# Two spectra and three norms: the second filters' folds and the sums of squares moved to VectorE

## The chip, the cores and the metric

The kernel runs on one core of a Trainium2 chip. The metric is the device time of one execution in microseconds, the median over the runs. All times below are microseconds unless marked ns. Engines: PE is TensorE, DVE is VectorE, ACT is ScalarE, POOL is GpSimd, SP is SyncE.

## What is computed

Two blocks of two layers each, all in float32, over 512 tokens of width 1024 and 256 context tokens. Both layers of the first block are attention layers with three kinds of heads. In the second block layer 0 (the "even" layer) joins a gated linear recurrence with long convolutions, layer 1 is a conformer convolution, and each is followed by 16 experts that choose their tokens. Ahead of every layer, of the experts and of the output stands a norm:

```python
def _rmsnorm(x, g):
    xf = x.astype(jnp.float32)
    y = xf * lax.rsqrt(jnp.mean(xf * xf, axis=-1, keepdims=True) + EPS)
    return (y * g.astype(jnp.float32)).astype(x.dtype)
```

The long convolutions of the even layer go through spectra, twice, each time with a filter of its own (o is 0 and 1) that a small network makes:

```python
def _fftconv(u, kf, bias):
    n = u.shape[1]
    uf = u.astype(jnp.float32)
    y = jnp.fft.irfft(jnp.fft.rfft(uf, n=2 * n, axis=1) * kf[None], n=2 * n, axis=1)[:, :n]
    return (y + uf * bias.astype(jnp.float32)).astype(u.dtype)
...
    z = v
    for o in range(HYENA_ORDER):
        z = gates[o] * _fftconv(z, kf[:, o], p['filt_bias'][o])
```

## The kernel before

The program is written by hand, engine by engine, with semaphores. Activations lie with channels on the partitions: XC holds the state (8 tiles of 128 channels by 768 tokens), HT the normed input of a layer. TensorE writes its results into two large PSUM buffers, BIG0 and BIG1, in turn; each use waits until the use before the last has been freed (`big_free`). A float32 matmul of 512 columns stands in the trace as two records of 128x512.

**A norm** (`norm`, `root_of_mean` on ScalarE, `norm_sums`, `square_sums`, `all_sums` on TensorE). While a layer's output projection runs, VectorE adds each tile, gated, to XC (`add_gated`, L1870; for four tiles of the even layer L2177), and ScalarE squares the tile into HT (L1471). TensorE sums the squares over the channels in groups of 32 output rows (`square_sums`), ScalarE copies that to RS (L1480), TensorE sums once more with ones (L863 for 512 columns, L865 for the 256 of the context), ScalarE takes the logarithm (L1483) and the exponential (L1487), VectorE scales (L1860) and ScalarE adds the shift (L1494). `keep_clock` puts matmuls without use between (L804). The norm behind the first attention layer has 768 tokens, those behind the second and behind the even layer 512.

**The spectra** (`even_layer`). The transform of real input is made in an even and an odd half, for two groups g of frequencies and two waves, cosine and sine, so in four matmul groups of 1024 columns, one use of BIG each (`transform`). "Folding" adds and subtracts the halves. TensorE's order is:

- filters and their spectrum for o = 0, filters for o = 1;
- the signal's spectrum (four uses), then the spectrum of the filters for o = 1 (four uses, the raw halves), since the tables are loaded then;
- four transforms back (`back_to_tokens`), the first of which waits for three of four spectral products (`spec_ready`), the third for the fourth;
- the signal to tokens again, the signal's spectrum (four uses), a part of the output projection into other banks (`partial`), four transforms back.

For the signal's spectrum ScalarE copies the even half to TA (`first_halves`, L1662) and VectorE folds it with the odd half in PSUM (`fold`, L2118 and L2119). After all four folds VectorE makes four products of ten operations each (`signal_spectrum`, L2139 to L2149), for g and half 0 and 1. Behind every transform back it adds and gates (`back_to_tokens`, L2158 and L2161).

The raw halves for o = 1 go from BIG to UT, a buffer in HT, by ScalarE (`raw_spectrum`, L1680), and from there GpSimd folds them (L742, L743) into two other places, in the weight ring and in the context part of XC, which the products of o = 1 read. UT holds two at a time, so ScalarE waits for GpSimd from the third on, and again before UT takes the signal's tokens.

The deleted lines of the diff below show these folds.

SyncE loads the weights in units of 1 MiB into a ring; a load waits for `unit_used`, which TensorE raises with the first matmul after a unit's last use (`mm`). The stage of the experts streams its weights through a ring of 16 such units.

## Time and profile before

| what | value |
|---|---|
| median of three runs | 3146.27 us (3146.1 to 3153.19) |
| the profiled execution, its own time | 3150.18 us |
| its span, first to last instruction | 3148.1 us |
| PE busy | 2958.5 us, 94% |
| DVE busy | 1236.6 us, 39% |
| ACT busy | 781.8 us, 25% |
| POOL busy | 92.9 us, 3% |
| mean granted clock of TensorE | 0.985 of full speed |

The profile counts an engine as busy while one of its instructions runs. A row of the timeline gives the start, the busy time, engine, line, operation, tiles and shapes, and in brackets how long the engine had been idle and what released it. Rows of one line that follow each other are merged ("x16"), and then the busy time is that of all. The granted clock is 1.00 at 2.4 GHz and 0.50 at 1.2 GHz. The even layer's spectra lie between 1730 and 1876 us, the three norms that are changed at 874, 1512 and 1917 us.

### The profile page before, as it was taken

Reading aid. Unit: us, or ns where it says so; the run is one execution under the profiler, and the core shown is the slowest. Engines: PE = TensorE matmul, PEld = TensorE weight load, DVE = VectorE, ACT = ScalarE, POOL = GpSimd, SP = SyncE. Lnnn points to the kernel's source line nnn. Section 1 sums busy time; section 2 is a strip of 40 time slices with the busy share of each in tenths; the row PEclk is TensorE's granted clock in tenths of the full one; section 3 lists DMA queues with packets and bytes.
Section 4 is the critical chain, followed back from the end, with each engine's and each line's share of the span. In section 5 each row is a group of like instructions: output and inputs, shape, how many; then the busy total and the mean of one; then the engine's idle time right before and its main releaser. Section 6 shows DMA issues by size and latency. Waiting matters only on the chain.

```text
span 3148.1 us, 33763 instructions
## 1 busy us (share of the span) xinstructions
PE 2958.5 (94%) x13428; PEld 1535.1 (49%) x13428; DVE 1236.6 (39%) x2397; ACT 781.8 (25%) x1370; POOL 92.9 (3%) x164
## 2 busy tenths in 40 slices
PE   7999988999999989999998799999999998999998
PEld 3556555655555555554443354444443434444442
DVE  1455564675024556681356653111112543111112
ACT  3223444332022245341343102010012122010011
POOL 0000000000000000010000100000000000000000
PEclk9999999999999999999999999999999999999999
DMA  6222221223112323233111014999997224999996
GB/s 263 72 92 72 79 87 61 68 79 122 67 53 100 125 90 125 87 122 136 54 67 40 15 67 187 410 421 421 422 420 305 73 76 172 405 421 421 421 421 283
DMA packets 90525, 584.47 MB, mean 186 GB/s; under 512 B 10176, under 2 KB 10176, under 8 KB 29216
## 3 DMA queue, kind: packets, MB, share of 16 engines
q1 hardware_dynamic: 69696, 502.56, 39.9%
q0 software_dynamic: 20704, 80.16, 7.9%
q8 instruction: 89, 1.46, 0.2%
q14 instruction: 36, 0.29, 0.0%
HBM read 580.58 MB, written 2.10 MB: 185 GB/s over the span
## 4 chain that ended last, share of the span: by engine, by line
PE 84%; DVE 9%; ACT 5%; issue 1%; DMA 1%; DVEq 0%; SPq 0%; ACTq 0%; POOL 0%
PE BIG L755 46%; PE PJ L755 21%; PE BIG L1412 4%; PE PJ L1010 3%; PE PT L989 3%; PE BIG L972 2%; PE BIG L976 1%; DVE SPILL L1845 1%; ACT ARENA L1572 1%; ACT ARENA L1562 1%; DVE STAT L1981 1%; PE PT L755 1%; PE PT L1388 0%; DMA W<-in_units 0%; ACT ARENA L1517 0%
## 5 line engine op out<-in xcount | busy, mean ns | idle before, releaser
L755 PE MATMUL PJ<-HT,W 128*128 128x512 f32 (+1 forms) x1792 | 648.0, 515 | 22.6 <-ACT ARENA L1544 11.0
L755 PE MATMUL BIG<-ARENA 128*64 128x512 f32 (+1 forms) x2368 | 474.3, 465 | 4.8 <-DVE ARENA L2266 2.5
L755 PEld LDWEIGHTS PJ<-HT,W 128*128 128x128 f32 x1792 | 337.3, 193 | 279.2 <-issue 240.5
L755 PEld LDWEIGHTS BIG<-ARENA 128*64 128x64 f32 (+1 forms) x2368 | 236.2, 165 | 230.7 <-issue 223.9
L755 PE MATMUL BIG<-HT,W 128*128 128x512 f32 (+1 forms) x768 | 321.0, 579 | 5.5 <-DVE CONST L2027 3.6
L755 PE MATMUL BIG<-W,ARENA 128*64 128x512 f32 (+1 forms) x1280 | 285.6, 576 | 18.4 <-DVE ARENA L2149 18.3
L755 PE MATMUL BIG<-ARENA,W 128*128 128x512 f32 (+1 forms) x768 | 289.7, 539 | 1.5 <-ACT ARENA L1729 1.5
L1572 ACT ACTIVATE ARENA<-PT 128x512 f32<-128x512 f32 (+1 forms) x280 | 150.0, 571 | 467.8 <-PE PT L989 466.5
L2295 DVE SCALAR_TENSOR_TENSOR XC<-BIG,MOD,XC 128x512 f32<-128x512 f32 x128 | 90.2, 747 | 379.6 <-PE BIG L1412 379.6
L755 PEld LDWEIGHTS BIG<-HT,W 128*128 128x128 f32 x768 | 146.8, 192 | 177.3 <-issue 166.5
L1845 DVE CUSTOM_DVE_ANT_0 SPILL<-W,VEC 128x1024 bf16<-128x1024 f32 x168 | 215.2, 1281 | 7.6 <-DMA W<-in_mod_rows 1.6
L755 PEld LDWEIGHTS BIG<-ARENA,W 128*128 128x128 f32 x768 | 145.7, 190 | 143.9 <-issue 138.2
L755 PEld LDWEIGHTS BIG<-W,ARENA 128*64 128x64 f32 (+1 forms) x1280 | 110.1, 144 | 179.6 <-issue 172.6
L1562 ACT ACTIVATE ARENA<-BIG,STAT 128x768 f32<-128x768 f32 (+6 forms) x240 | 174.0, 730 | 61.4 <-DVE STAT L1981 60.6
L1981 DVE TENSOR_REDUCE STAT<-BIG 128x1 f32<-128x768 f32 (+6 forms) x240 | 174.1, 742 | 29.0 <-PE BIG L976 24.0
L989 PE MATMUL PT<-CONST,ARENA 128*128 128x128 f32 x1056 | 155.8, 282 | 17.3 <-ACT ARENA L1572 16.1
L755 PE MATMUL BIG<-HT,ARENA 128*64 128x512 f32 x576 | 169.7, 592 | 0.0
L1010 PEld LDWEIGHTS PJ<-ARENA 128*64 128x64 f32 x2112 | 113.9, 136 | 84.3 <-issue 46.8
L1010 PE MATMUL PJ<-ARENA 128*64 128x128 f32 x2112 | 142.9, 278 | 9.9 <-DVE ARENA L1890 4.4
L989 PEld LDWEIGHTS PT<-CONST,ARENA 128*128 128x128 f32 x1056 | 112.1, 140 | 72.1 <-issue 38.6
L1935 DVE TENSOR_SCALAR ARENA<-ARENA,STAT 128x512 f32<-128x512 f32 (+3 forms) x240 | 123.5, 515 | 8.4
L1412 PE MATMUL BIG<-ARENA 128*128 128x512 f32 x256 | 115.0, 602 | 0.0
(254 smaller groups left out, 2188.9 us busy)
## 6 DMA issues: line engine op xcount, KB each, us to landing
ARENA<-in_exp_w SPq DMA_DIRECT2D x168, 1024.0 KB, 18.2
W<-in_exp_w SPq DMA_DIRECT2D x144, 1024.0 KB, 16.8
W<-in_units SPq DMA_DIRECT2D x89, 1024.0 KB, 4.9
HT<-in_exp_w SPq DMA_DIRECT2D x72, 1024.0 KB, 22.0
W<-in_mod_rows POOLq DMA_DIRECT2D x128, 512.0 KB, 3.9
ARENA<-in_bias_b POOLq DMA_DIRECT2D x16, 448.0 KB, 5.6
XC<-in_x SPq DMA_DIRECT2D x1, 3072.0 KB, 10.3
W<-in_mod_vectors POOLq DMA_DIRECT2D x2, 1024.0 KB, 6.2
```

The lines of the kernel that those rows point to most:

```text
L755: ins = pe.matmul(out, lhsT, rhs, start=start, stop=stop)
L972: pe.matmul(BIG[h][:, N - (b - a) * P:N], Q[rows, i % 2, t * P:t * P + P], keys[rows, a * P:b * P], start=True, stop=True)
L976: pe.matmul(BIG[h][:, N:NA], Q[rows, i % 2, t * P:t * P + P], keys[rows, N:NA], start=True, stop=True).then_inc(scores_filled, 1)
L989: last = pe.transpose(PT[:, a:a + P], PROB[:, h, y * P:y * P + P], const("ident"))
L1010: last = pe.matmul(PJ[use_o[0]][head * HD:head * HD + HD, 0:P], V[:, buf_of[i], tile, head * HD:head * HD + HD], PTS[:, at:at + P], start= ...
L1412: last = pe.matmul(BIG[k_use % 2][:, half * N:half * N + N], YK[:, m * P:m * P + P], GSCAT[:, :], start=True, stop=True)
L1562: act.activation(PROB[:, h, 0:b - a], BIG[h][:, a:b], ACT.Exp, bias=STAT[:, c:c + 1], accum_out=STAT[:, 4 + c:5 + c]).then_inc(probs_exp, 1)
L1572: act.activation(PTS[:, a:a + w], PT[:, bank:bank + w], ACT.Copy).then_inc(t_copied, 1)
L1845: dve.tensor_tensor_reduce(SPILL[:, :], MODW[:, row % 2, :], MODV[:, which, :], 1.0, vec("mod_b", at), ALU.mult, ALU.add, MOD[:, at:at + 1 ...
L1935: dve.tensor_scalar(probs, probs, STAT[:, 8 + c:9 + c], None, ALU.mult)\
L1981: dve.tensor_reduce(STAT[:, c:c + 1], out[:, a:b], AX.X, ALU.max, negate=True).then_inc(max_ready, 1)
L2295: ins = dve.scalar_tensor_tensor(XC[:, m, 0:N], BIG[k_use % 2][:, half * N:half * N + N], mod(group, 5, m, 0), XC[:, m, 0:N], ALU.mult, AL ...
```

## The change

It has two parts.

**Folds.** ScalarE evicts the raw halves straight to the two places in the weight ring and in XC (now RAW_COS and RAW_SIN), without waits on another engine. GpSimd's folds are deleted. VectorE folds them (`fold_raw`) behind the four gatings of o = 0, into KR and KS, the places of the first filters' spectrum, so both products read the same tiles. `signal_spectrum` folds group 0, makes the first product, and only then folds group 1; it does so for both o.

**Norms.** For the three norms named above VectorE adds up the squares in HT as they come (`add_squares`): behind the gating of tile m it adds the square of tile m-2 (the sum so far) to that of tile m-1. TensorE sums only two tiles, the running sum and the last square, with ones of full width (`summed_squares`). The copy to RS and the second sum go. The other norms stay.

```diff
         LRU_W = W[:, RING, :].rearrange("p (g n) -> p g n", n=P)
-        SPEC_R1 = W[:, RING, :].rearrange("p (g s w n) -> p g w s n", g=2, s=2, w=2)
-        SPEC_S1 = XC[:, :, N:NA].rearrange("p (g s w) n -> p g w s n", g=2, s=2)
+        RAW_COS = W[:, RING, :].rearrange("p (g s w n) -> p g s w n", g=2, s=2, w=2)
+        RAW_SIN = XC[:, :, N:NA].rearrange("p (g s w) n -> p g s w n", g=2, s=2)
         FILT_W3 = W[:, RING + 1, :]
...
         DFT_IN, DFT_OUT = (W[:, hyena_slots[x], :].rearrange("p (a k b) -> p a k b", a=4, k=2) for x in (1, 2))
-        SPECTRA = [[x.rearrange("p g s (w n) -> p g w s n", w=2) for x in (KR, KS)], [SPEC_R1, SPEC_S1]]
+        SPECTRUM = [x.rearrange("p g s (w n) -> p g w s n", w=2) for x in (KR, KS)]
...
-            for x in range(4):
-                g, wave = divmod(x, 2)
-                even, odd = (UT[:, 2 * (x % 2) + part, :].rearrange("p (w n) -> p w n", w=2) for part in range(2))
-                plus, minus = (SPECTRA[1][wave][:, g, :, s, :] for s in range(2))
-                pool.wait_ge(raw_copied, x + 1)
-                pool.tensor_tensor(plus, even, odd, ALU.add)
-                pool.tensor_tensor(minus, odd if wave else even, even if wave else odd, ALU.subtract)\
-                    .then_inc(raw_folded, 1)
...
+            def summed_squares(n):
+                k_use = me.next_big()
+                pe.wait_ge(big_free[k_use % 2], me.over(k_use - 2))
+                out = BIG[k_use % 2]
+                for k in (KT - 2, KT - 1):
+                    if k == KT - 2:
+                        pe.wait_ge(squares_added, me.next("squares_added"))
+                        me.next("squares", KT)
+                    else:
+                        pe.wait_ge(squares, me.seen["squares"])
+                    last = mm(out[:, 0:N], const("ones"), HT[:, k, 0:N], k == KT - 2, k == KT - 1)
+                if n > N:
+                    for k in (KT - 2, KT - 1):
+                        last = pe.matmul(out[:, N:n], const("ones"), HT[:, k, N:n], start=k == KT - 2, stop=k == KT - 1)
+                last.then_inc(big_filled, 1)
...
                     act.activation(HT[:, k, 0:n], XC[:, k, 0:n], ACT.Square).then_inc(squares, 1)
-                root_of_mean(n)
+                root_of_mean(n, summed)
                 if shift is not None:
...
-            def root_of_mean(n):
-                k_use = me.next_big()
-                act.wait_ge(big_filled, me.fills(k_use))
-                act.activation(RS[:, 0:n], BIG[k_use % 2][:, 0:n], ACT.Copy).then_inc(big_free[k_use % 2], 1)
+            def root_of_mean(n, summed=False):
+                if not summed:
+                    k_use = me.next_big()
+                    act.wait_ge(big_filled, me.fills(k_use))
+                    act.activation(RS[:, 0:n], BIG[k_use % 2][:, 0:n], ACT.Copy).then_inc(big_free[k_use % 2], 1)
                 k_use = me.next_big()
...
                 act.activation(RS[:, 0:n], BIG[k_use % 2][:, 0:n], ACT.Ln, bias=EPSC[:, 0:1],
-                               scale=1.0 / (32 * D))\
+                               scale=1.0 / (D if summed else 32 * D))\
                     .then_inc(big_free[k_use % 2], 1)
...
                     for x in range(4):
+                        g, wave = divmod(x, 2)
+                        raw = (RAW_COS, RAW_SIN)[wave][:, g].rearrange("p s w n -> p (s w) n")
                         k_use = me.next_big()
                         act.wait_ge(big_filled, me.fills(k_use))
-                        if x >= 2:
-                            act.wait_ge(raw_folded, x - 1)
-                        act.activation(UT[:, 2 * (x % 2):2 * (x % 2) + 2, :],
-                                       BIG[k_use % 2][:, :].rearrange("p (a b) -> p a b", b=N), ACT.Copy)\
+                        act.activation(raw, BIG[k_use % 2][:, :].rearrange("p (a n) -> p a n", n=256), ACT.Copy)\
                             .then_inc(big_free[k_use % 2], 1)
-                        act.wait_ge(big_free[k_use % 2], me.over(k_use)).then_inc(raw_copied, 1)
...
                 me.big += 4
-                act.wait_ge(raw_folded, 4)
                 signal_tokens()
...
-            def norm(n, weight, group, scale_chunk, dst, done):
+            def add_squares(n, m, before):
+                if m >= 2:
+                    dve.wait_ge(squares, before + m)
+                    ins = dve.tensor_tensor(HT[:, m - 1, 0:n], HT[:, m - 1, 0:n], HT[:, m - 2, 0:n], ALU.add)
+                    if m == KT - 1:
+                        ins.then_inc(squares_added, 1)
+                    else:
+                        link(ins)
+            def norm(n, weight, group, scale_chunk, dst, done, summed=False):
...
                                                       1.0, weight, ALU.add, ALU.mult))
-                me.big += 2
+                me.big += 1 if summed else 2
                 dve.wait_ge(rs_ready, me.next("rs_ready"))
...
                     ins.then_inc(big_free[k_use % 2], 1)
+                    add_squares(n, m, before)
...
-                def signal_spectrum(o):
-                    for g in range(2):
+                def fold_raw(first_use):
+                    for x in range(4):
+                        g, wave = divmod(x, 2)
+                        even, odd = ((RAW_COS, RAW_SIN)[wave][:, g, s, :, :] for s in range(2))
+                        plus, minus = ((KR, KS)[wave][:, g, s, :].rearrange("p (w n) -> p w n", w=2) for s in range(2))
+                        dve.wait_ge(big_free[(first_use + x) % 2], me.over(first_use + x))
+                        dve.tensor_tensor(plus, even, odd, ALU.add)
+                        ins = dve.tensor_tensor(minus, odd if wave else even, even if wave else odd, ALU.subtract)
+                    link(ins)
+                def signal_spectrum():
+                    def folds(g):
...
+                    folds(0)
                     for g in range(2):
                         for half in range(2):
+                            if (g, half) == (0, 1):
+                                folds(1)
                             part = slice(half * 256, half * 256 + 256)
-                            kr, ks = (SPECTRA[o][wave][:, g, half, :, :] for wave in range(2))
+                            kr, ks = (SPECTRUM[wave][:, g, half, :, :] for wave in range(2))
                             ur, us, zt, zr = (x[:, :, part] for x in (UR[g], US[g], ZT, ZR))
...
                 filters()
-                signal_spectrum(0)
+                signal_spectrum()
+                first_use = me.big
                 me.big += 4
                 back_to_tokens(0)
+                fold_raw(first_use)
                 me.big += 2
-                dve.wait_ge(raw_folded, 4)
-                signal_spectrum(1)
+                signal_spectrum()
                 back_to_tokens(1)
...
                                              ALU.mult, ALU.add).then_inc(partial_added, 1)
-                add_gated(N, lambda m, c: mod(2, 2, m, c), range(4, KT))
+                    add_squares(N, m, SQUARES_BEFORE["even"])
+                add_gated(N, lambda m, c: mod(2, 2, m, c), SQUARES_BEFORE["even"], range(4, KT))
```

What moves on the engines shows in the orders. First VectorE at the signal's spectrum of o = 0, before, from the second of its four pairs of folds (L2118, L2119) to the start of the first product (L2139, L2140); UR, US and KR lie in ARENA:

```order
L2118 TENSOR_TENSOR ARENA<-ARENA,BIG1 128x512 [waits half_copied,big_free0]
L2119 TENSOR_TENSOR ARENA<-BIG1,ARENA 128x512
L2118 TENSOR_TENSOR ARENA<-ARENA,BIG0 128x512 [waits half_copied,big_free1]
L2119 TENSOR_TENSOR ARENA<-ARENA,BIG0 128x512
L2118 TENSOR_TENSOR ARENA<-ARENA,BIG1 128x512 [waits half_copied,big_free0]
L2119 TENSOR_TENSOR ARENA<-BIG1,ARENA 128x512
L2139 TENSOR_TENSOR ARENA<-ARENA 128x2x256 [waits big_free1]
L2140 TENSOR_TENSOR ARENA<-ARENA 128x2x256
```

And in the changed kernel, the end of the first product (L2183 to L2186), the second two pairs of folds (L2139 and L2140 there), and the start of the second product (L2176):

```order
L2183 TENSOR_TENSOR ARENA<-ARENA 128x256 [waits dve_chain]
L2184 TENSOR_TENSOR ARENA<-ARENA 128x256
L2185 TENSOR_TENSOR ARENA<-ARENA 128x256
L2186 TENSOR_TENSOR ARENA<-ARENA 128x256
L2139 TENSOR_TENSOR ARENA<-ARENA,BIG0 128x512 [waits half_copied,spec_ready]
L2140 TENSOR_TENSOR ARENA<-ARENA,BIG0 128x512
L2139 TENSOR_TENSOR ARENA<-ARENA,BIG1 128x512 [waits half_copied,big_free0]
L2140 TENSOR_TENSOR ARENA<-BIG1,ARENA 128x512
L2176 TENSOR_TENSOR ARENA<-ARENA 128x2x256 [waits big_free1]
L2177 TENSOR_TENSOR ARENA<-ARENA 128x2x256
```

The two folds of group 1, which free BIG0 and BIG1 for the raw transforms, have moved behind ten operations. The second place is VectorE between the last gating of o = 0 and the next signal spectrum, before:

```order
L2158 SCALAR_TENSOR_TENSOR ARENA<-ARENA,VEC,BIG0 128x2x256 [waits big_filled]
L2161 TENSOR_TENSOR ARENA<-ARENA 128x512 [waits dve_chain]
L2158 SCALAR_TENSOR_TENSOR ARENA<-ARENA,VEC,BIG1 128x2x256 [waits big_filled]
L2161 TENSOR_TENSOR ARENA<-ARENA 128x512 [waits dve_chain]
L2118 TENSOR_TENSOR ARENA<-ARENA,BIG0 128x512 [waits half_copied,raw_folded]
L2119 TENSOR_TENSOR ARENA<-ARENA,BIG0 128x512
```

and in the changed kernel (L2195 and L2198 are the gating, L2157 and L2158 the new folds, W and XC where the raw halves lie):

```order
L2195 SCALAR_TENSOR_TENSOR ARENA<-ARENA,VEC,BIG1 128x2x256 [waits big_filled]
L2198 TENSOR_TENSOR ARENA<-ARENA 128x512 [waits dve_chain]
L2157 TENSOR_TENSOR ARENA<-W 128x512 [waits big_free0]
L2158 TENSOR_TENSOR ARENA<-W 128x512
L2157 TENSOR_TENSOR ARENA<-XC 128x512 [waits big_free1]
L2158 TENSOR_TENSOR ARENA<-XC 128x512
L2157 TENSOR_TENSOR ARENA<-W 128x512 [waits big_free0]
L2158 TENSOR_TENSOR ARENA<-W 128x512
L2157 TENSOR_TENSOR ARENA<-XC 128x512 [waits big_free1]
L2158 TENSOR_TENSOR ARENA<-XC 128x512
L2139 TENSOR_TENSOR ARENA<-ARENA,BIG0 128x512 [waits half_copied,dve_chain]
```

Eight additions of 512 columns now stand there. The third place is TensorE at the norm behind the first attention layer (PJ and BIG are PSUM, CONST holds the ones), before:

```order
L755 MATMUL BIG<-ARENA,W 128x256 x12
L755 MATMUL BIG<-HT,CONST 32x512 x8
L755 MATMUL BIG<-HT,CONST 32x256 x8
L863 MATMUL BIG<-ARENA,CONST 128x512
L865 MATMUL BIG<-ARENA,CONST 128x256
L804 MATMUL PJ<-CONST 128x512 x5
L755 MATMUL PJ<-HT,W 128x512 x8
```

and in the changed kernel:

```order
L748 MATMUL BIG<-ARENA,W 128x256 x12
L748 MATMUL BIG<-HT,CONST 128x512 x2
L845 MATMUL BIG<-HT,CONST 128x256 x2
L797 MATMUL PJ<-CONST 128x512 x5
L748 MATMUL PJ<-HT,W 128x512 x8
```

Sixteen narrow sums and two wide ones have become four wide ones.

## Rows read from the trace of the kernel before

**Rows 1.** The page, busy time of each engine.
```profile
PE 2958.5 (94%) x13428; PEld 1535.1 (49%) x13428; DVE 1236.6 (39%) x2397; ACT 781.8 (25%) x1370; POOL 92.9 (3%) x164
```
**Rows 2.** Timeline of VectorE, first signal spectrum: start, busy time, engine, line, operation, tiles.
```profile
1775.10 0.68 DVE L2119 TENSOR_TENSOR ARENA<-BIG,ARENA 128x512 f32<-128x512 f32 x1
...
1782.67 0.69 DVE L2139 TENSOR_TENSOR ARENA<-ARENA 128x512 f32<-128x512 f32 x1
...
1785.34 1.75 DVE L2143 TENSOR_TENSOR ARENA<-ARENA 128x512 f32<-128x512 f32 x1
...
1801.84 0.69 DVE L2139 TENSOR_TENSOR ARENA<-ARENA 128x512 f32<-128x512 f32 x1
...
1807.41 0.69 DVE L2139 TENSOR_TENSOR ARENA<-ARENA 128x512 f32<-128x512 f32 x1
```
**Rows 3.** Timeline of GpSimd, first and last of its eight folds.
```profile
1785.24 1.30 POOL L742 TENSOR_TENSOR W<-HT 128x512 f32<-128x512 f32 x1 [240.89 <-ACTq L1683]
...
1796.75 1.71 POOL L743 TENSOR_TENSOR XC<-HT 128x512 f32<-128x512 f32 x1
```
**Rows 4.** Timeline of all engines, first spectrum and the transforms back.
```profile
1780.65 0.60 ACT L1662 ACTIVATE ARENA<-BIG 128x512 f32<-128x512 f32 x1 [2.84 <-PE BIG L755]
...
1807.52 16.29 PE L755 MATMUL BIG<-W,ARENA 128*128 128x256 f32 x64 [13.17 <-DVE ARENA L2149]
...
1813.56 0.75 DVE L2158 SCALAR_TENSOR_TENSOR ARENA<-ARENA,VEC,BIG 128x512 f32<-128x512 f32 x1 [0.61 <-PE BIG L755]
...
1816.94 0.75 DVE L2158 SCALAR_TENSOR_TENSOR ARENA<-ARENA,VEC,BIG 128x512 f32<-128x512 f32 x1 [1.91 <-PE BIG L755]
...
1823.85 0.75 DVE L2158 SCALAR_TENSOR_TENSOR ARENA<-ARENA,VEC,BIG 128x512 f32<-128x512 f32 x1 [1.98 <-PE BIG L755]
...
1831.92 0.69 DVE L2118 TENSOR_TENSOR ARENA<-ARENA,BIG 128x512 f32<-128x512 f32 x1 [6.60 <-ACT ARENA L1662]
```
**Rows 5.** Windows: stretch, its length, busy time by engine, granted clock, DMA share, GB/s.
```profile
1807.50:1811.00 3.50, 3.48 (x8) 2.83 (x9) 3.40 (x6) 0.00 (x0) 0.00 (x0) 0.50 0.30 61
```
**Rows 6.** Timeline of the second spectrum, VectorE's second fold, and the transforms back.
```profile
1835.96 0.68 DVE L2119 TENSOR_TENSOR ARENA<-BIG,ARENA 128x512 f32<-128x512 f32 x1
...
1860.38 15.47 PE L755 MATMUL BIG<-W,ARENA 128*128 128x256 f32 x64 [5.16 <-DVE ARENA L2149]
...
1875.89 0.75 DVE L2158 SCALAR_TENSOR_TENSOR ARENA<-ARENA,VEC,BIG 128x512 f32<-128x512 f32 x1 [1.98 <-PE BIG L755]
```
**Rows 7.** Timeline of the norm with 768 tokens; last, VectorE's group of 768 columns.
```profile
874.16 1.14 DVE L1870 SCALAR_TENSOR_TENSOR XC<-BIG,MOD,XC 128x512 f32<-128x512 f32 x2 [14.34 <-PE BIG L755]
...
875.33 0.84 ACT L1471 ACTIVATE HT<-XC 128x768 f32<-128x768 f32 x1 [14.64 <-DVE XC L1870]
...
879.04 1.13 PE L863 MATMUL BIG<-ARENA,CONST 128*128 128x512 f32 x2 [0.90 <-ACT ARENA L1480]
...
880.63 0.90 ACT L1483 ACTIVATE ARENA<-BIG,EPSC 128x768 f32<-128x768 f32 x1 [0.35 <-PE BIG L865]
...
L2047 DVE TENSOR_TENSOR ARENA<-ARENA 128x768 f32<-128x768 f32 x8 | 7.7, 958 | 8.3 <-ACT ARENA L1633 8.2
```
**Rows 8.** Timeline of the norm behind the second attention layer, 512 tokens.
```profile
1512.60 0.75 DVE L1870 SCALAR_TENSOR_TENSOR XC<-BIG,MOD,XC 128x512 f32<-128x512 f32 x1 [9.55 <-PE BIG L755]
...
1515.80 1.13 PE L863 MATMUL BIG<-ARENA,CONST 128*128 128x512 f32 x2 [0.69 <-ACT ARENA L1480]
...
1517.06 0.69 ACT L1483 ACTIVATE ARENA<-BIG,EPSC 128x512 f32<-128x512 f32 x1
```
**Rows 9.** Timeline of TensorE, two gaps elsewhere.
```profile
1294.56 5.85 PE L755 MATMUL PJ<-HT,W 128*128 128x512 f32 x13 [2.33 <-DVE ARENA L1952]
...
1658.14 1.79 PE L1030 MATMUL BIG<-ARENA,W 128*128 128x512 f32 x2 [2.29 <-ACT ARENA L1625]
```
**Rows 10.** The experts: SyncE's queue behind the even layer, and a window of the stage.
```profile
1918.43 26.12 SPq L633 DMA_DIRECT2D ARENA<-in_exp_w  x7
...
2025.00:2075.00 50.00, 50.00 (x254) 22.55 (x250) 5.07 (x7) 5.55 (x6) 0.00 (x0) 1.00 1.01 420
```

More of the change, by code:

```diff
@@ L192, in unit_order @@
     return first, second
+SQUARES_BEFORE = {"attention": [KT, 2 * KT], "even": 4 * KT}
 class Count:
@@ L479, in build @@
         squares = sem("squares")
+        squares_added = sem("squares_added")
         rs_ready = sem("rs_ready")
@@ L525, in build @@
         y_half_copied = sem("y_half_copied")
-        raw_copied = sem("raw_copied")
-        raw_folded = sem("raw_folded")
         partial_done = sem("partial_done")
@@ L1436, in _ @@
             attention(0)
-            norm_sums(NA)
+            summed_squares(NA)
             keep_clock(5)
             attention(1)
-            norm_sums(N)
+            summed_squares(N)
             keep_clock(4)
@@ L1444, in _ @@
             even_layer()
-            norm_sums(N)
+            summed_squares(N)
             keep_clock(4)
@@ L1459, in _, with norm @@
             me = Count()
-            def norm(n, updates, shift, follow=None):
+            def norm(n, updates, shift, follow=None, summed=False):
                 for k in range(KT):
@@ L1800, in _ @@
             updates = attention(0)
-            norm(NA, updates, lambda k, c: mod(1, 0, k, c))
+            norm(NA, updates, lambda k, c: mod(1, 0, k, c), summed=True)
             updates = attention(1)
-            norm(N, updates, None)
+            norm(N, updates, None, summed=True)
             act.wait_ge(ctx2_loaded, 16)
@@ L1807, in _ @@
             updates = even_layer()
-            norm(N, updates, lambda k, c: mod(2, 3, k, c))
+            norm(N, updates, lambda k, c: mod(2, 3, k, c), summed=True)
             updates = experts(0)
@@ L1861, in norm, with add_gated @@
                                                  ALU.mult, ALU.mult).then_inc(done, 1)
-            def add_gated(n, gates, tiles=range(KT)):
+            def add_gated(n, gates, before, tiles=range(KT)):
                 for m in tiles:
@@ L1945, in attention @@
                 dve.wait_ge(mod_made, MODS_DONE[0])
-                add_gated(nq, lambda m, c: mod(layer, 2, m, c))
+                add_gated(nq, lambda m, c: mod(layer, 2, m, c), SQUARES_BEFORE["attention"][layer])
             def values(kv, part, use):
@@ L2316, in _ @@
                     dve.wait_ge(mod_made, MODS_DONE[1])
-                norm(NA, vec("norm_w", 8 * layer, 8), layer, 1, HT, h_scaled)
+                norm(NA, vec("norm_w", 8 * layer, 8), layer, 1, HT, h_scaled, summed=layer == 1)
                 attention(layer)
-            norm(N, vec("final_norm_w", 0, 8), None, None, XC, block_done)
+            norm(N, vec("final_norm_w", 0, 8), None, None, XC, block_done, summed=True)
             dve.wait_ge(block_done, KT)
@@ L2332, in _ @@
             even_layer()
-            norm(N, vec("norm2_g", 0, 8), 2, 4, HT, h_scaled)
+            norm(N, vec("norm2_g", 0, 8), 2, 4, HT, h_scaled, summed=True)
             experts(0)
```

## The prediction

> **What bounds the kernel now.** I read the page first: TensorE is busy for 2958.5 us of a span of 3148.1 us [rows 1]. Work taken off another engine therefore counts only where TensorE stands still for it. The second view is the timeline of VectorE, GpSimd, ScalarE and TensorE around the two signal spectra and around each norm; the third is the same stretch in windows, for the granted clock. The two edits touch five places: the first and second spectrum, and three norms. Times below are those of the trace of before.
>
> **First spectrum, before.** VectorE folds the four signal transforms as they arrive and then makes four products of ten operations. The third product takes from 1801.84 to 1807.41, 5.57 us [rows 2]. The first two together take from 1782.67 to 1801.84, 19.17 us, where two at 5.57 are 11.14: 8.03 us are lost. The long operations (1.75 us at 1785.34, where its like takes 0.69) stand exactly where GpSimd folds the raw halves, 1785.24 to 1798.46 [rows 2, 3]. TensorE must have three products: it has nothing to do for 13.17 us and goes on at 1807.52 [rows 4]. The clock granted in the 3.5 us behind that is 0.50, the lower level of 1.2 GHz [rows 5]. In the end four transforms back, 3.455 us apart at full speed (1816.94 to 1823.85), need 16.33 us from 1807.52 to the eviction of the fourth, where 4 x 3.455 + 0.1 = 13.9 would do.
>
> **First spectrum, changed.** GpSimd's folds are gone, so every product costs 5.57 us. The order is new too: the first product is made before the second pair of folds. The second fold ends at 1775.10 + 0.68 = 1775.78 [rows 2]. Then: product 1 to 1781.35; two folds of 0.61 + 0.68 to 1783.95; products 2 and 3 to 1795.1; product 4 to 1800.7. This adds a wait. The buffer of the third transform is freed by its fold at 1782.65, and TensorE wants it for the first raw transform when the fourth is done, at 1780.55 (ScalarE copies its half at 1780.65) [rows 4]. So TensorE stalls for 2.2 us, and behind it stand the four raw transforms, now ending at 1807.52 - 13.17 = 1794.35 and then at 1796.55. That is later than the third product (1795.1), so TensorE itself is what comes last, and it goes on at 1796.6: 10.9 us earlier. Without the 13 us of standing still the clock should stay up, so 16.33 becomes 13.9: 2.4 us more. **Gain 13.3 us.** The fourth product (1800.7) delays nothing: the third transform back, which needs it, starts at 1803.5.
>
> **The folds, now on VectorE.** Eight additions of 512 columns at 0.61 us apart (0.69 at most, from the two rows of a fold) are 4.9 to 5.6 us. They follow the last gating; there VectorE has been idle for 6.60 us before 1831.92 [rows 4]. Hidden, cost 0, with 1.0 to 1.7 us to spare. If that cover were gone, each microsecond would delay the second spectrum. ScalarE loses three waits and no work: a copy of 1024 columns to another place. GpSimd loses eight operations that nothing else follows on its queue.
>
> **Second spectrum.** Only the order changes. The second fold ends at 1836.64 [rows 6]; product 1 to 1842.2, folds to 1844.8, products 2 and 3 to 1856.0. TensorE goes on then, at 1856.1, not at 1860.38; it has been free since 1860.38 - 5.16 = 1855.2. That is 4.3 us. From 1860.38 to the fourth eviction at 1875.89 are 15.51 us, against 13.9 at full speed: 1.6 us more if 0.9 us of waiting leaves the clock alone. The fourth product ends at 1861.6, so the first gating frees its buffer at 1863.2, 0.2 us after the third transform could have started. **Gain 5.7 us.**
>
> **Three norms.** Before, ScalarE's last square is followed by sums on TensorE, a copy, a second sum and the logarithm. With 768 tokens the last gating ends at 875.30 and the logarithm starts at 880.63 [rows 7]. Now VectorE adds squares behind each gating; the six additions ahead of the last hide in the 14 us between gatings. The last, of 768 columns, takes 0.96 us (the nearest row, L2047) and ends at 876.28; the last square runs beside it, 875.33 to 876.17. TensorE starts at 876.36. Now 879.04 to 880.63, 1.59 us, is one sum of 512 and one of 256 columns with the way to ScalarE. Columns of 512 are two records of 0.43 us, those of 256 half as much, so two sums each need 1.59 + 0.86 + 0.43 = 2.88 us: logarithm at 879.24. **Gain 1.4 us.** With 512 tokens the gating ends at 1513.35, the addition at 1514.05, TensorE starts at 1514.15 and needs 1.26 + 0.86 = 2.12 us: 1516.27 instead of 1517.06 [rows 8]. **Gain 0.8 us, twice.** The matmuls that keep the clock up end 1.5 us sooner with the rest, so they don't become the bound. ScalarE's table load of 1.28 us stays under TensorE's sums.
>
> One DMA is moved with it: the release of the last output unit hangs on the first sum, which now waits for the additions. The loads of expert weights that follow it started at 1918.43 [rows 10], before the last gating ended at 1917.84 + 0.69; they will start about 1 us later against the gating. The queue issues these seven over 26.12 us and a microsecond hides in that; cost 0.
>
> **Sum.** 13.3 + 5.7 + 1.4 + 0.8 + 0.8 = 22.0 us. Against it stand two new gaps of 2.2 us on TensorE, at the first raw transform and ahead of the sums of the norm with 768 tokens. Of such gaps the trace shows both kinds: after 2.33 us at 1294.56 records come 0.45 us apart (5.85 us for 13); after 2.29 us at 1658.14 two records take 1.79 us [rows 9]. A fall costs about 1.7 us if it lasts as long as the 3.5 us at half speed in [rows 5], nothing if only the matmuls that keep the clock up run in it. I take one fall of the two, -1.7 us: **20.3 us gained**. The Trainium skill, "TensorE: Matmul & The Clock Gate", section "HAM oscillation", lets the clock fall only after longer standing still than these gaps; by that rule the sum would be 22.0. The row at 1658.14 speaks against it, so I keep 20.3.
>
> The profiled execution took 3150.18 us, its span 3148.1; it is 3.9 above the median of the runs, 3146.27, whose own spread is 7 us. It would become 3129.9, the median **3126.0 us**.
>
> **Rivals.**
> The products stay slow (0.07): it may be ScalarE's evictions of the four raw transforms that slow VectorE, not GpSimd. For it: they lie in the same stretch. Against it: the slow operations stop with GpSimd's last, and the gatings and folds of the second spectrum, with ScalarE evicting between them, run at full speed. Then the third product ends 8.0 us later, at 1803.1, TensorE stands for 6.6 us, the clock falls as before, and the first spectrum gains 4.3: 13.0 in all, 3133.3 us. The Trainium skill, "SBUF — State Buffer", section "Who interferes with whom", has only VectorE and GpSimd share a port; by it this rival would have no chance.
>
> The folds don't hide (0.05): were the eight additions as slow as the long ones (1.65 us), they would need 13.2 us against 6.6 of cover, and 6.6 come back: 15.4 less 1.7 gained, 3132.6 us. Nothing but GpSimd made them slow, so it is unlikely.
>
> The experts take it back (0.06): beside them the DMA queues are full (share 1.01, 420 GB/s) while TensorE is busy for 50.00 of 50 us [rows 10]. If the stream of weights set the end, it would still start with the same release, which comes some 19 us earlier; lost are the last norm's 0.8 and the 1 us of delay: 3127.8 us.
>
> Slower (0.02): the clock. If the fall behind a new gap did not end after some microseconds but held through the stretch of attention or of the transforms that follows, then each microsecond at 1.2 GHz loses half of one. To end 9.4 us above before it must eat 22.0 + 9.4 = 31.4 us, that is 63 us at the lower level: about 3156 us. From 44 us on the gain is gone. The 3.5 us of [rows 5] are the kind of length that the trace has, so this is a remote case.
>
> No change worth the name (0.03): a mix of these with a late wait that I don't see, say another operand of the transforms back; the gain of the first spectrum would be lost, 3139 us or more.
>
> **Numbers.** A measurement can tell about 0.3%, 9.4 us. My case has 0.77 and lies between 3124 (no fall) and 3128 (two). The range takes in the 22.0 with some microseconds of the runs' spread below, and the first rivals above: 3120.5 to 3133.5. Faster by over 0.3% (under 3136.8) is 0.95, within it 0.03, slower 0.02.
>
> **What would show it.** Right: all products at 5.6 us; TensorE's wait ahead of the transforms back gone in the first spectrum and about 1 us in the second; a new wait of 2.2 us at the first raw transform, released by a fold; eight additions between the last gating and the next fold with 1 to 2 us idle behind; the logarithm 3.9 us after the last gating with 768 tokens, 2.9 us with 512. Wrong: products above 0.7 us per operation with GpSimd idle, a TensorE wait over 2 us ahead of the transforms back, or stretches at 1.2 GHz behind the new gaps that last longer than those of before.

## The result and the profile after

Seven runs of the changed kernel have a median of 3133.2 us (3127.32 to 3141.46); seven of the kernel before, on the same chip and in turn with them, 3153.19 us (3145.71 to 3154.79). The first three of these seven are the three behind the median of 3146.27 us that the prediction started from. The ratio is 0.9946, 95% interval 0.993 to 0.9962: 17 us less, 12 to 22. The profiled execution took 3131.21 us with a span of 3129.2; that of the kernel before took 3150.18 with a span of 3148.1, 19 us more.

The page of the changed kernel, span and busy time of each engine, against [rows 1]:

```profile
span 3129.2 us, 33675 instructions
## 1 busy us (share of the span) xinstructions
PE 2951.6 (94%) x13372; PEld 1532.3 (49%) x13372; DVE 1245.7 (40%) x2423; ACT 779.8 (25%) x1367; POOL 81.2 (3%) x156
```

TensorE is busy 6.9 us less and the span is 18.9 us shorter: most of what went was standing still.

**First spectrum.** Timeline of VectorE, ScalarE and TensorE in the changed kernel; columns are start, busy time, engine, line, operation and tiles, in brackets the idle time before and what ended it. L2139 and L2140 are the folds of the signal, L2176 the first operation of a product, L2195 a gating, L2157 and L2158 the folds of the raw halves. The rows are picked from the three engines, so rows between them are left out:

```profile
1775.35 0.68 DVE L2140 TENSOR_TENSOR ARENA<-BIG,ARENA 128x512 f32<-128x512 f32 x1
1776.07 0.69 DVE L2176 TENSOR_TENSOR ARENA<-ARENA 128x512 f32<-128x512 f32 x1
1781.64 0.69 DVE L2139 TENSOR_TENSOR ARENA<-ARENA,BIG 128x512 f32<-128x512 f32 x1
1782.98 14.00 PE L748 MATMUL BIG<-HT,W 128*128 128x512 f32 x32 [2.11 <-DVE ARENA L2140]
1784.29 0.69 DVE L2176 TENSOR_TENSOR ARENA<-ARENA 128x512 f32<-128x512 f32 x1
1789.86 0.69 DVE L2176 TENSOR_TENSOR ARENA<-ARENA 128x512 f32<-128x512 f32 x1
1795.44 0.69 DVE L2176 TENSOR_TENSOR ARENA<-ARENA 128x512 f32<-128x512 f32 x1
1796.82 13.98 PE L748 MATMUL BIG<-W,ARENA 128*128 128x256 f32 x64
1810.83 0.75 DVE L2195 SCALAR_TENSOR_TENSOR ARENA<-ARENA,VEC,BIG 128x512 f32<-128x512 f32 x1 [1.98 <-PE BIG L748]
1812.22 0.68 DVE L2157 TENSOR_TENSOR ARENA<-W 128x512 f32<-128x512 f32 x1
1816.44 0.69 DVE L2158 TENSOR_TENSOR ARENA<-XC 128x512 f32<-128x512 f32 x1
```

Products start 5.57 us apart (1784.29, 1789.86, 1795.44), where the first two took 19.17 together [rows 2]. TensorE no longer stands still ahead of the transforms back: its row at 1796.82 has no bracket, where [rows 4] have 13.17 us. In its place is the wait of 2.11 us at the first raw transform, ended by a fold (the third of the signal's four, the one at 1781.64). From the start of the second fold (1775.35, before 1775.10) to the fourth gating (1810.83, before 1823.85) are 35.48 us instead of 48.75: **13.27 us gained**.

**Second spectrum.** The same views, from the first fold on the signal to the fourth gating:

```profile
1818.84 0.69 DVE L2139 TENSOR_TENSOR ARENA<-ARENA,BIG 128x512 f32<-128x512 f32 x1 [1.71 <-ACT ARENA L1674]
1822.88 0.68 DVE L2140 TENSOR_TENSOR ARENA<-BIG,ARENA 128x512 f32<-128x512 f32 x1
1843.07 14.17 PE L748 MATMUL BIG<-W,ARENA 128*128 128x256 f32 x64 [0.94 <-DVE ARENA L2186]
1857.28 0.75 DVE L2195 SCALAR_TENSOR_TENSOR ARENA<-ARENA,VEC,BIG 128x512 f32<-128x512 f32 x1 [1.98 <-PE BIG L748]
```

The eight new additions leave VectorE idle for 1.71 us, where it had 6.60 [rows 4]: they are hidden. TensorE waits for 0.94 us instead of 5.16 [rows 6]. Second fold to fourth gating is 34.40 us, before 1875.89 - 1835.96 = 39.93: **5.53 us gained**.

**The norms.** With 768 tokens; L1890 is the gating, L1862 the addition of squares, L1495 the logarithm:

```profile
874.39 1.14 DVE L1890 SCALAR_TENSOR_TENSOR XC<-BIG,MOD,XC 128x512 f32<-128x512 f32 x2 [13.47 <-PE BIG L748]
875.45 0.95 DVE L1862 TENSOR_TENSOR HT<-HT 128x768 f32<-128x768 f32 x1
876.55 3.08 PE L748 MATMUL BIG<-HT,CONST 128*128 128x512 f32 x4 [2.26 <-DVE HT L1862]
879.42 1.64 PE L845 MATMUL BIG<-HT,CONST 128*128 128x256 f32 x4
881.10 0.90 ACT L1495 ACTIVATE ARENA<-BIG,EPSC 128x768 f32<-128x768 f32 x1 [3.39 <-PE BIG L845]
```

The same, with 512 tokens (the norm behind the second attention layer):

```profile
1512.89 0.75 DVE L1890 SCALAR_TENSOR_TENSOR XC<-BIG,MOD,XC 128x512 f32<-128x512 f32 x1 [8.95 <-PE BIG L748]
1514.38 1.96 PE L748 MATMUL BIG<-HT,CONST 128*128 128x512 f32 x4 [1.60 <-DVE HT L1862]
1516.38 0.69 ACT L1495 ACTIVATE ARENA<-BIG,EPSC 128x512 f32<-128x512 f32 x1 [0.77 <-PE BIG L748]
```

With 512 tokens the logarithm starts 3.49 us after the start of the gating, before 1517.06 - 1512.60 = 4.46 [rows 8]: 0.97 us gained, and as much at the norm behind the even layer. With 768 tokens it starts after 6.71 us, before 880.63 - 874.16 = 6.47 [rows 7]: **0.24 us lost**. The four records of 512 columns that take 1.96 us at 1514.38 take 3.08 at 876.55. The window shows why; columns are the stretch, its length, busy time of PE, PEld, DVE, ACT and POOL with the instructions of each, the granted clock, the DMA share and GB/s:

```profile
877.00:884.00 7.00, 7.00 (x16) 3.50 (x15) 0.00 (x0) 3.58 (x4) 0.00 (x0) 0.76 0.44 150
```

The clock fell behind the gap of 2.26 us, for about half of these 7 us. At the other new gap of 2 us it did not:

```profile
1779.00:1790.00 11.00, 8.89 (x22) 3.75 (x21) 10.66 (x21) 1.62 (x2) 0.00 (x0) 1.00 0.01 1
```

**The balance of the two traces.** 13.27 + 5.53 + 0.97 + 0.97 - 0.24 = 20.5 us at the five places. The spans differ by 18.9, so 1.6 us was lost in stretches whose code is the same. The largest piece lies between the logarithm of the norm at 1516 us and the second fold at 1775: 258.97 us, before 258.04.

### The profile page after: what moved, and what is told of

Its sections match the earlier page's. It is cut to its first block, busy times and chain, and to the rows that moved or that the text cites. A ratio compares the mean times of both kernels' runs of the same rounds, so it can differ in the third digit from the quotient of the medians.

```text
span 3129.2 us, 33675 instructions
## 1 busy us (share of the span) xinstructions
PE 2951.6 (94%) x13372; PEld 1532.3 (49%) x13372; DVE 1245.7 (40%) x2423; ACT 779.8 (25%) x1367; POOL 81.2 (3%) x156
## 4 chain that ended last, share of the span: by engine, by line
PE 84%; DVE 8%; ACT 5%; issue 2%; DMA 1%; DVEq 0%; SPq 0%; POOL 0%; ACTq 0%
PE BIG L748 46%; PE PJ L748 20%; PE BIG L1423 4%; PE PJ L1021 3%; PE PT L1000 3%; PE BIG L983 2%; PE BIG L987 1%; DVE SPILL L1854 1%; ACT ARENA L1584 1%; ACT ARENA L1574 1%; DVE STAT L2002 1%; PE PT L748 1%; PE PT L1399 1%; DMA ARENA<-in_bias_b 0%; DMA W<-in_units 0%
```

## Experiments: which edit gives what

Four kernels were run in one session, six executions of the first and twelve of each of the others; 29 executions of the kernel before beside them have a median of 3149.34 us. For each is also told what its trace shows at the five places, counted as above. The ratios have intervals of 0.13 to 0.22 points either way, some 4 to 7 us.

**Folds alone**: the changed kernel with the norms as before.

```diff
-            summed_squares(NA)
+            norm_sums(NA)
...
-            norm(NA, updates, lambda k, c: mod(1, 0, k, c), summed=True)
+            norm(NA, updates, lambda k, c: mod(1, 0, k, c))
...
-                if m >= 2:
+                if False:
```

> Only the spectra are changed, all norms as before. If the waits are what the prediction says, 13.3 + 5.7 = 19.0 us less than before (range 15 to 20), with a wait of 2.1 us at the first raw transform and none ahead of the transforms back of the first spectrum. If the products had not become faster by GpSimd's leaving, about 10 us.

Measured: 3129.11 us, ratio 0.9936 (0.9914 to 0.9958). Its trace has both spectra as the changed kernel has them (first: second fold at 1769.48, fourth gating at 1804.97, 35.49 us) and all norms as before. Its local gain is 18.8 us of the 20.5 of the whole change. In whole executions the rest can't be told: the mean of these six is 3130.1 us, that of all 18 of the changed kernel 3129.1.

**Norms alone**: the kernel before with the norms' hunks of the change.

> Only the three norms are changed, the spectra as before. Theory 1 (the sum of waits): 1.4 + 0.8 + 0.8 = 3.0 us less than before. Theory 2 (the gap that VectorE's last addition leaves on TensorE lets the clock fall): about 1.3 us less on average, 3.0 where the clock stays up behind the norm with 768 tokens and 1.3 or less where it falls.

Measured: 3147.48 us, ratio 0.9986 (0.9973 to 1.0). The sign can barely be told. TensorE's timeline at the norm with 768 tokens again has the gap of 2.26 us with slow sums behind it:

```profile
875.60 3.29 PE L759 MATMUL BIG<-HT,CONST 128*128 128x512 f32 x4 [2.26 <-DVE HT L1876]
878.68 1.43 PE L856 MATMUL BIG<-HT,CONST 128*128 128x256 f32 x4
```

With 512 tokens gating to logarithm is 3.49 us, as in the changed kernel. By the trace the three norms give 0.97 + 0.97 - 0.24 = 1.7 us, not the 3.0 of the sum of waits.

**VectorE's folds in the old order**: folds alone, and both groups folded ahead of the first product.

```diff
                     folds(0)
+                    folds(1)
                     for g in range(2):
                         for half in range(2):
-                            if (g, half) == (0, 1):
-                                folds(1)
```

> Norms as before; the raw halves folded by VectorE as in the change, but all four folds of the signal ahead of the first product as before. If GpSimd's reads slowed VectorE, every product takes 5.6 us, the third ends 16.7 us after the first begins, and TensorE waits 5.1 us instead of 13.2: 8 to 10 us less than before, and nothing from the second spectrum. If ScalarE's evictions slowed it: products at 9.6 us still and 0 to 1 us less than before.

Measured: 3142.53 us, ratio 0.9971 (0.9958 to 0.9985). It parts GpSimd's work from the order, and tests the rival that ScalarE's evictions slow the products. Timeline of all engines: two raw copies by ScalarE, the first operations of three products, and the transforms back.

```profile
1789.33 0.69 DVE L2175 TENSOR_TENSOR ARENA<-ARENA 128x512 f32<-128x512 f32 x1
1790.74 1.02 ACT L1692 ACTIVATE W<-BIG 128x1024 f32<-128x1024 f32 x1 [2.83 <-PE BIG L748]
1794.17 1.02 ACT L1692 ACTIVATE XC<-BIG 128x1024 f32<-128x1024 f32 x1 [2.41 <-PE BIG L748]
1794.90 0.69 DVE L2175 TENSOR_TENSOR ARENA<-ARENA 128x512 f32<-128x512 f32 x1
1800.47 0.69 DVE L2175 TENSOR_TENSOR ARENA<-ARENA 128x512 f32<-128x512 f32 x1
1806.16 15.44 PE L748 MATMUL BIG<-W,ARENA 128*128 128x256 f32 x64 [5.16 <-DVE ARENA L2185]
```

Products take 5.57 us with ScalarE's copies in the middle of them, so that rival is out for these copies (into W and XC; before, ScalarE copied as many columns to HT). TensorE's wait falls from 13.17 to 5.16 us: 8.01, the 8.03 us that the products had lost. The transforms back still take 15.44 us behind the wait, as those of the second spectrum before did behind the same 5.16 [rows 6].

**The new order with GpSimd's folds**: the kernel before, with `folds(1)` behind the first product as in the change.

> Norms as before; GpSimd still folds the raw halves, only the order is changed (first product before the second pair of folds, for both spectra). If GpSimd slows VectorE for 8 us wherever it runs: third product 4.4 us earlier in the first spectrum, plus 5.7 us in the second: 9 to 11 us less than before. If ScalarE slowed VectorE the same, so this run is not to tell these two apart but to tell how much the order alone is worth, and whether the slow operations follow GpSimd's when they move by some microseconds.

Measured: 3138.8 us, ratio 0.9963 (0.9951 to 0.9976). Timeline of GpSimd (first and last of eight), VectorE and TensorE:

```profile
1782.39 1.61 POOL L742 TENSOR_TENSOR W<-HT 128x512 f32<-128x512 f32 x1 [239.89 <-ACTq L1683]
1794.13 1.71 POOL L743 TENSOR_TENSOR XC<-HT 128x512 f32<-128x512 f32 x1
...
1782.18 0.69 DVE L2149 TENSOR_TENSOR ARENA<-ARENA 128x512 f32<-128x512 f32 x1
1782.91 1.37 DVE L2151 TENSOR_TENSOR ARENA<-ARENA 128x256 f32<-128x256 f32 x1
1789.03 0.68 DVE L2145 TENSOR_TENSOR ARENA<-ARENA 128x512 f32<-128x512 f32 x1
1792.97 1.75 DVE L2148 TENSOR_TENSOR ARENA<-ARENA 128x512 f32<-128x512 f32 x1
1796.42 0.42 DVE L2151 TENSOR_TENSOR ARENA<-ARENA 128x256 f32<-128x256 f32 x1
1798.00 16.86 PE L755 MATMUL BIG<-W,ARENA 128*128 128x256 f32 x64 [6.50 <-DVE ARENA L2154]
```

VectorE's slow operations begin and end with GpSimd's (the first slow one starts at 1782.91, the last at 1794.75), and the operation at 1789.03, which starts while GpSimd pauses, is quick. The order alone takes the wait from 13.17 to 6.50 us and gives the second spectrum all that it has in the change (34.40 us). The transforms back need 16.86 us behind the wait, so the first spectrum as a whole gains 3.72 us.

The two parts of the first spectrum do not add. The transforms back start 8.0 us sooner with VectorE's folds in the old order and 4.3 by the order alone (from ScalarE's copy of the fourth half, 1780.65 before: 26.87 us; here 1775.42 to 1798.00, 22.58), and 10.95 by both (1780.90 to 1796.82, 15.92). About 1.4 us are missing. They are TensorE's own raw transforms, which the wait of 2.11 us holds up, the cap that the prediction had put in; the early fold below takes that wait away and gets 1.0 of them back.

## Experiments: the gaps and the clock

Four kernels, in a second session with nine executions of the kernel before (median 3149.32 us), and two in a third (eleven, 3150.91 us). The two sessions ran on two different chips.

**The same change again**, unaltered.

> The changed kernel once more, for more executions. The first seven gave a mean of 3133.5 us at a mean clock of 0.9869. If the gains of the two parts add up (about 20 for the spectra, 3 to 4 for the norms), its mean must come out 3 us below that of the spectra alone (3130.1), near 3127, and the seven were drawn low on the clock. If the norms' gap costs more clock than it saves work, it stays at 3131 to 3134.

> The changed kernel as it stands, a third time, to see which of two readings of 17.0 us and 27.4 us of gain in its first two sets of runs holds. If the gain is the sum of local gains of the trace (13.3 + 5.5 + 1.0 + 1.0 - 0.2 = 20.5 us) and the rest is the clock that an execution happens to be granted (2.4 us per 0.001 of its mean), the median comes out 20.5 us under the kernel before, 3 us either way: about 3128.5 to 3129.5 us against 3149.3, and the executions line up with their clocks. If the change itself lets the clock fall more often (rival), the mean clock of its executions is under that of the kernel before and the gain stays at 17 us or less.

Measured: 3121.94 us, ratio 0.9916 (0.9903 to 0.993), and then 3129.1 us, ratio 0.9926 (0.9909 to 0.9942). With the first set three medians of one kernel: 3133.2, 3121.94 and 3129.1. The second lies 11 us from the first, and the intervals of their ratios only touch, at 0.993. The chip doesn't explain it: the second and third set differ by 7 us, the kernel before beside them by 1.6. Yet the five places are alike in the three traces: the first spectrum takes 35.48 us in each, the logarithm with 768 tokens starts 6.71, 6.68 and 6.63 us after the gating. What differs is the granted clock: its mean over the executions of a set is 0.9869, 0.9902 and 0.9887, slowest with the slowest. The same stretch of code shows how, 11.7 us in attention behind a gap of 2.52 us; first the changed kernel as first profiled:

```profile
313.30:325.00 11.70, 9.18 (x66) 8.98 (x66) 2.30 (x5) 5.97 (x9) 0.00 (x0) 0.85 0.01 1
```

and the same stretch in the run of it that followed, at its place there:

```profile
314.00:325.70 11.70, 9.18 (x81) 8.93 (x80) 3.71 (x7) 6.03 (x9) 0.00 (x0) 1.00 0.00 1
```

The traces have 17 gaps of over 1.9 us on TensorE. Within the 6 us behind a gap the granted clock fell at 12 of them in the first of these traces and at 10 in the second, but not at the same ones. Over the 130 executions of these sets and of the kernel before beside them, with each kernel given its own level, a line fits the time to 1.9 us with 2.5 us for each 0.001 of mean clock. That is a correlation; no run set the clock.

**The gaps ahead of the norms' sums filled** with matmuls that nothing reads:

```diff
             def summed_squares(n):
...
+                keep_clock(2 if n > N else 1)
                 k_use = me.next_big()
```

> The change with matmuls without use in the two kinds of new gaps at the norms (two at the norm with 768 tokens, one at each with 512). Theory 2, the gap at the norm lets the clock fall in about half of the executions: the fall behind that norm is gone, mean clock about 0.0005 higher, 1 to 2 us less than the change. If the clock there plays no part: 0 us, or up to 0.5 more where a filler ends late.

> The changed kernel with TensorE's two-microsecond gap ahead of each norm's sums filled by matmuls that nothing reads, again, beside the changed kernel on the same chip. If the fall of the clock behind the gap of 2.26 us at the norm with 768 tokens comes every time, filling it gives 1.7 us there (logarithm 5.0 us after the start of the gating instead of 6.7), and the median lies 0 to 4 us under the changed kernel's. If that fall is one of chance and something else falls in its place, the two medians agree within 2 us and the fall shows in some traces of the changed kernel only.

Measured: 3127.67 us, ratio 0.9927 (0.9912 to 0.9941), and in the third session 3128.67 us, ratio 0.9923 (0.9908 to 0.9939). TensorE and ScalarE at the norm with 768 tokens:

```profile
873.92 1.88 PE L797 MATMUL PJ<-CONST 128*128 128x512 f32 x4
874.20 1.14 DVE L1891 SCALAR_TENSOR_TENSOR XC<-BIG,MOD,XC 128x512 f32<-128x512 f32 x2 [13.47 <-PE BIG L748]
876.35 1.96 PE L748 MATMUL BIG<-HT,CONST 128*128 128x512 f32 x4 [0.54 <-DVE HT L1863]
878.14 1.03 PE L846 MATMUL BIG<-HT,CONST 128*128 128x256 f32 x4
879.20 0.90 ACT L1496 ACTIVATE ARENA<-BIG,EPSC 128x768 f32<-128x768 f32 x1 [1.69 <-PE BIG L846]
```

and the window:

```profile
876.50:883.50 7.00, 6.96 (x18) 3.15 (x18) 1.13 (x2) 4.38 (x5) 0.00 (x0) 1.00 0.44 150
```

The sums start 2.15 us after the gating's start in this trace and 2.16 in the changed kernel's; what differs is how long they take. The slow sums stand in all five traces that have the gap and in none of the three with the gap filled. Gating to logarithm is 5.00 us instead of 6.71 (5.01 in the second set). So at this norm the new sums do give 6.47 - 5.00 = 1.47 us, and the fall behind the gap takes 1.71. In whole executions that can't be seen: the eleven of this kernel have a mean of 3127.8 us, the 18 of the changed kernel 3129.1, which themselves spread by 5.7 us (standard deviation).

**The third fold early**: behind the third operation of the first product instead of behind the tenth, so that a buffer comes free for the first raw transform.

```diff
                             if (g, half) == (0, 1):
-                                folds(1)
+                                folds(1, (1,))
...
                             link(dve.tensor_tensor(zr, zr, zt, ALU.subtract))
+                            if (g, half) == (0, 0):
+                                folds(1, (0,))
```

> The change with the third fold of the signal moved into the first product, behind its third operation, so that the buffer is free before TensorE wants it. The sum of waits says: no wait of 2.1 us at the first raw transform, the transforms back start 1.4 us earlier (the third product, 0.8 us later than TensorE, becomes the bound): 1.4 us less than the change. If that gap also cost the clock: 2 to 3 us less. If the wait only moves elsewhere: 0.

Measured: 3128.84 us, ratio 0.9934 (0.992 to 0.9947). In TensorE's timeline the wait at the raw transform is gone (the matmuls of both transforms stand in one row, 48 of them inside the view's window) and a shorter one comes ahead of the transforms back, which now wait for the third product:

```profile
1771.79 21.09 PE L748 MATMUL BIG<-HT,W 128*128 128x512 f32 x48
1793.55 14.17 PE L748 MATMUL BIG<-W,ARENA 128*128 128x256 f32 x64 [0.67 <-DVE ARENA L2189]
```

From the second fold (1773.30) to the fourth gating (1807.75) are 34.45 us, 1.03 less than in the changed kernel. That gain is local; in the median it doesn't show. The fall at the norm with 768 tokens stays, as this run doesn't touch that gap.

**Both** the early fold and the filled gaps.

> Both of these together: 2.5 to 4 us less than the change, 20 to 27 us less than the kernel before, if both gaps count; it should then be the fastest of all.

Measured: 3125.32 us, ratio 0.9925 (0.9911 to 0.9938). By its trace it keeps both gains (34.45 us in the first spectrum, 5.01 at the norm), 2.7 us in all. Its interval overlaps those of the changed kernel, so it isn't shown to beat it.

The local gains against the means of whole executions (the kernel before: 3150.65 us over 49):

| kernel | executions | mean us | gain | gain at the five places |
|---|---|---|---|---|
| changed, three sets | 18 | 3129.1 | 21.5 | 20.5 |
| folds alone | 6 | 3130.1 | 20.6 | 18.8 |
| norms alone | 12 | 3146.2 | 4.4 | 0.4 |
| VectorE's folds, old order | 12 | 3142.5 | 8.1 | 7.6 |
| new order, GpSimd's folds | 12 | 3138.0 | 12.7 | 9.3 |
| gaps filled, two sets | 11 | 3127.8 | 22.9 | 22.2 |
| early fold | 5 | 3129.1 | 21.5 | 21.5 |
| both | 5 | 3125.6 | 25.1 | 23.2 |

The last column is from the one profiled execution of each (the changed kernel's first). In those of norms alone and of the old order the second spectrum, whose code is as before, took 1.6 and 1.3 us longer than there, which is counted. Every row agrees within 4 us; the spread of 3 to 5 us among the executions of a kernel leaves 1 to 2 to their mean, and a single trace has its own falls of the clock, so a difference of this size isn't a contradiction.

## Why the prediction was partly right and partly wrong

**The mechanism and the sum were right.** The prediction had 20.3 us gained. The trace has 20.5 at the five places, and 18 executions against 49 have 21.5 in their means.

- First spectrum, 13.3 predicted, 13.27 found. Its parts are shown one by one: the products' 8.0 us were GpSimd's doing, the new order gives the rest, and TensorE is the cap (10.95 us sooner, 10.9 predicted). The other 2.3 us (2.4 predicted) are the transforms back, which no longer start at the lower clock: 14.01 us to the fourth gating instead of 16.33.
- The folds on VectorE, 0 predicted with 1.0 to 1.7 us to spare; 1.71 us are left.
- Second spectrum, 5.7 predicted, 5.53 found; the wait that stays is 0.94 us, 0.9 predicted, and the clock stands at 1.00 from 1818 to 1870 us. The transforms back need 14.2 us to the fourth gating instead of 13.9.
- Norms with 512 tokens, 0.8 each predicted, 0.97 found. VectorE makes six additions at a norm, so five go ahead of the last and not six, which changes no term.
- The load of expert weights. It starts at 1901.54 us, 2.99 us after the start of the last gating (1898.55). The prediction misread the kernel before here: 1917.84 us is where its last gating ends, not where it starts (1917.09), so the load came 1.34 us after that start, and the delay is 1.65 us, not 1. The seven issues are out 23.49 us later, at 1925.03. Before that was 1918.43 + 26.12 = 1944.55 [rows 10]: 19.5 us sooner, as much as the logarithm. The delay vanished in the queue, cost 0 as predicted. In SyncE's queue:

```profile
1901.54 23.49 SPq L635 DMA_DIRECT2D ARENA<-in_exp_w  x7
```

- One clock fall of two, -1.7 us. That came out to the tenth (1.71), but that it would be one, and not none or both, was a guess, and in this the sum had luck. It was put down as a fall of chance, one gap or the other. In the runs it has a fixed place: the gap of 2.26 us at the norm with 768 tokens fell in all five traces that have it (the changed kernel's three, norms alone, early fold), the gap of 2.11 us at the raw transform in none of seven. So the term "Gain 1.4 us" of the norm is worth nothing in this kernel (-0.24 us), and the spectra keep all of theirs. The sign "the logarithm 3.9 us after the last gating with 768 tokens" did not come: it is 881.10 - 875.53 = 5.57 us. By the Trainium skill's rule that the prediction weighed ("TensorE: Matmul & The Clock Gate", section "HAM oscillation"), neither gap should have cost anything; the windows at 877 us (0.76) and, filled, at 876.5 us (1.00) show that this one did.

**What failed is the level.** The step reads "It would become 3129.9, the median **3126.0 us**". The profiled execution became 3131.21, 1.3 us off. The median came out at 3133.2, 7 us off, at the upper edge of the range and outside the 3124 to 3128 us that the main case was given. By the ratio of its session it would be 3146.27 x 0.9946 = 3129.3. The gain was taken off a median of three runs, 3146.27, of which two (3146.1 and 3146.27) lay at the lower edge of what this kernel does: 49 later executions reach from 3145.22 to 3163.28 us with a median of 3149.6. Their mean, 3150.65, less the predicted gain is 3130.4, and the 18 executions of the changed kernel have 3129.1. So of the miss 4.4 us are the base; the other part is that the first seven executions of the changed kernel drew a low clock (mean 3133.5 us at 0.9869, 4.4 us above the mean of all 18), less the 1.2 us by which the gain was larger than forecast. This spread of whole executions is the term that was put at nothing on the upper side, and it belonged in the range. It was built from the bounds of the terms and the rivals, with "some microseconds of the runs' spread below" and none above, while the same kernel gave medians from 3121.94 to 3133.2 us.

**The rivals.** The products that stay slow, the folds that don't hide and the experts that take the gain back are excluded by the rows above; the fall that lasts did not come, the one at 877 us being over within the 7 us of the window. The claim that the change itself makes later stretches lose the clock is not borne out: in its three sets the mean clock is 0.9884, that of the kernel before 0.9858. The spectra alone account for this difference: the kernel before was granted 0.92 over their 100.8 us (1775.10 to 1875.90), which lowers the mean of its whole span by 0.0026 (0.08 x 100.8 of 3148 us), the changed kernel 1.00 over its 81.9 us. So the rest of the program is granted about the same clock in both.

**Open.** Why the clock fell behind the gap of 2.26 us in each of five traces and behind that of 2.11 in none of seven: their lengths, what TensorE did before and where they lie all differ, and no run parted these. Two gaps in code that is the same in all twelve traces have such habits too: the clock fell behind the one of 2.10 us at 707 us in none of them, behind the one of 2.32 us at 1695 us in eleven. Why other gaps fall in one execution and not in the next was not found either.

## What to carry to other kernels

Two engines that add and multiply in the same memory can cost more than the second engine saves. Here GpSimd's eight folds cost VectorE 8.0 us, and VectorE does the same eight in 4.9 (1812.22 to 1817.13). Look for operations that take more than twice as long as their like only while the other is busy, and count that loss against the move. Where the waited-for result is the third of four, order the work by who waits, and check which buffer the new order frees late: here both edits together were capped by such a wait. When several microseconds are at stake in a kernel with many short gaps, read the gain between fixed marks of two traces, and take the level from many executions, since from one execution to the next they move by more than that, together with their mean clock.

## What the runs showed of the hardware

- One program on one core, without any change, gave medians of 3121.94, 3129.1 and 3133.2 us in three sessions. Over 130 executions of nine kernels the time goes with the mean granted clock, 2.5 us for 0.001, and the gaps behind which the clock falls are in part others in each trace.
- A fall behind a gap of 2.26 us cost 1.71 us in the sums that follow, and four matmul records placed in the gap took all of it away at no cost: the sums started as early as without them.
- VectorE's operations of 512 columns take 1.63 to 1.75 us instead of 0.69 while GpSimd adds in the same stretch, those of 256 columns 1.37 to 1.49 instead of 0.42, and those that start while GpSimd pauses are quick (0.68 at 1789.03 in the new order with GpSimd's folds). ScalarE's copies of 1024 columns out of PSUM leave them at 0.69 (1789.33 to 1800.47 with VectorE's folds in the old order).
